# A two-block network on one core: how the conv half of a mixer layer gets its sum of squares

## The reference

```python
def rmsnorm(x, g):
    xf = x.astype(jnp.float32)
    y = xf * lax.rsqrt(jnp.mean(xf * xf, axis=-1, keepdims=True) + EPS)
    return (y * g.astype(jnp.float32)).astype(x.dtype)
...
        a = rmsnorm(h, mix_norm_g[i])
        proj = a @ w_in[i]
        q, k, v = (proj[..., 0:SB_WIDTH],
                   proj[..., SB_WIDTH:2 * SB_WIDTH],
                   proj[..., 2 * SB_WIDTH:3 * SB_WIDTH])
        off = 3 * SB_WIDTH
        u, c_gate, b_gate = (proj[..., off:off + CONV_WIDTH],
                             proj[..., off + CONV_WIDTH:off + 2 * CONV_WIDTH],
                             proj[..., off + 2 * CONV_WIDTH:off + 3 * CONV_WIDTH])
...
        qh = rmsnorm(heads(q), q_norm_g[i])
        kh = rmsnorm(heads(k), k_norm_g[i])
        vh = heads(v)
        attn = stick_breaking_attention(qh, kh, vh)
        attn = attn.transpose(0, 2, 1, 3).reshape(bsz, s_len, SB_WIDTH)

        conv = b_gate * causal_depthwise_conv(c_gate * u, conv_w[i], conv_b[i])

        mixed = jnp.concatenate([rmsnorm(attn, attn_out_g[i]),
                                 rmsnorm(conv, conv_out_g[i])], axis=-1)
        h = h + mixed @ w_o[i]
```

## Time and profile before

| | us |
|---|---|
| median of three runs | 1921.33 |
| lowest, highest | 1921.16, 1925.42 |
| the profiled execution, time | 1927.16 |
| the profiled execution, span | 1925.3 |
| PE busy in it | 1838.6 (95%) |
| DVE busy | 1395.7 (72%) |
| ACT busy | 1220.0 (63%) |

### The profile page before, as it was taken

One profiled execution on the slowest core, in us unless ns is written; L12 is line 12 of the kernel. 1 busy time (PEld: TensorE's weight loads), 2 busy tenths in 40 slices (PEclk: granted clock), 3 DMA queues, 4 the chain that ended last, 5 costly groups with the idle time before them and its releaser, 6 DMA issues.

```text
span 1925.3 us, 26803 instructions
## 1 busy us (share of the span) xinstructions
PE 1838.6 (95%) x9562; PEld 1546.2 (80%) x9562; DVE 1395.7 (72%) x1653; ACT 1220.0 (63%) x1536; POOL 5.9 (0%) x13
## 2 busy tenths in 40 slices
PE   8999979989999989879999999999999999999997
PEld 7877758979998779768878878788788787887885
DVE  4456755746664466458899898898998898989884
ACT  5545544644444455548687777786877777768773
POOL 0000000000000000000000000000000000000000
PEclk9889989999999999879999999999999999999999
DMA  9743223425445344219989899899898998998980
GB/s 321 248 165 109 74 102 131 154 100 190 177 190 202 111 175 176 93 67 339 369 319 362 317 364 364 310 367 355 325 361 319 352 360 325 358 345 343 357 323 23
DMA packets 68336, 483.32 MB, mean 251 GB/s; under 512 B 7610, under 2 KB 7738, under 8 KB 10928
## 3 DMA queue, kind: packets, MB, share of 16 engines
q1 hardware_dynamic: 66480, 475.26, 64.9%
q0 software_dynamic: 1792, 7.18, 1.8%
HBM read 478.22 MB, written 4.19 MB: 251 GB/s over the span
## 4 chain that ended last, share of the span: by engine, by line
PE 80%; DVE 8%; ACT 6%; issue 5%; DMA 0%; ACTq 0%; DVEq 0%; POOLq 0%
PE ps L1471 20%; PE ps L1472 19%; PE ps L1476 19%; DVE wlo L892 4%; PE ps L1716 4%; PE ps L1723 4%; PE ps L1717 4%; PE ps L1454 3%; ACT whi L549 2%; PE ps L1928 1%; PE ps L1929 1%; ACT xgh L846 1%; DVE sg L1015 1%; ACT sg L672 1%; PE ps L1819 1%
## 5 line engine op out<-in xcount | busy, mean ns | idle before, releaser
L892 DVE TENSOR_TENSOR wlo<-raw,whi 128x1024 fp32r<-128x1024 f32 x906 | 1044.1, 1212 | 171.8 <-ACT whi L549 171.3
L549 ACT ACTIVATE whi<-raw 128x1024 fp32r<-128x1024 f32 x906 | 904.2, 1055 | 154.6 <-PE ps L1476 127.4
L1471 PE MATMUL ps<-whi,xgh 128*128 128x512 f32 x896 | 360.2, 402 | 4.6 <-ACT whi L549 4.6
L1472 PE MATMUL ps<-whi,xgl 128*128 128x512 f32 x896 | 355.0, 396 | 0.0
L1476 PE MATMUL ps<-wlo,xgh 128*128 128x512 f32 x896 | 282.2, 396 | 0.0
L1471 PE MATMUL ps<-whi,xh 128*128 128x512 f32 (+1 forms) x448 | 186.9, 418 | 21.9 <-issue 9.9
L1471 PEld LDWEIGHTS ps<-whi,xgh 128*128 128x128 f32 x896 | 168.9, 188 | 43.1 <-ACT whi L549 4.8
L1476 PEld LDWEIGHTS ps<-wlo,xgh 128*128 128x128 f32 x896 | 168.9, 188 | 40.8
L1472 PEld LDWEIGHTS ps<-whi,xgl 128*128 128x128 f32 x896 | 169.2, 189 | 37.8
L1472 PE MATMUL ps<-whi,xl 128*128 128x512 f32 (+1 forms) x448 | 181.3, 406 | 0.0
L1471 PE MATMUL ps<-whi,mTh 128*128 128x512 f32 x448 | 178.3, 398 | 0.0
(11 more groups left out here) (288 smaller groups left out, 1902.5 us busy)
## 6 DMA issues: line engine op xcount, KB each, us to landing
raw<-in_w_moe_dram SPq DMA_DIRECT2D x336, 1024.0 KB, 6.7
raw<-in_w_fixed_dram SPq DMA_DIRECT2D x112, 1024.0 KB, 4.9
bias_scratch<-revb POOLq DMA_DIRECT2D x1, 3072.0 KB, 39.2
bias<-bias_scratch POOLq DMA_DIRECT2D x1, 2048.0 KB, 18.2
raw<-in_w_fixed_dram SPq DMA_DIRECT2D x4, 512.0 KB, 4.2
tok<-in_xt_dram SPq DMA_DIRECT2D x2, 512.0 KB, 4.5
h<-in_x_dram SPq DMA_DIRECT2D x1, 1024.0 KB, 13.6
out_dram<-h SPq DMA_DIRECT2D x2, 512.0 KB, 2.8
```

Source lines behind the costliest of these rows:

```text
L549: AC(whi[:, v % SPL, c], raw[:, v % RAW, c], ACT.Copy).then_inc(high_done, 1)
L892: V.tensor_tensor(wlo[:, v % SPL, c], raw[:, v % RAW, c], whi[:, v % SPL, c].bitcast(F32), ALU.subtract).then_inc(low_done, 1)
L1471: mm(o, hi(k0 + k, T), wh[:, k, :], start=first and k == 0, stop=False)
L1472: mm(o, lo(k0 + k, T), wh[:, k, :], start=False, stop=False)
```

## The change

DVE gets one more instruction per mixer layer. It adds up the four 128 x 256 tiles of conv squares to one tile `conv_squares` of 128 x 256, reading them with tokens outside and tiles inside (a step of 256 words, 1 KB, between the four values of one sum). It stands ahead of `low_part` on DVE, behind a wait for the squares. PE then sums this one tile over the features. The sums of the attention half stay as they are. `conv_squares` is a new buffer of 1 KB per partition, `conv_reduced` a new semaphore.

```diff
@@ -215,6 +215,7 @@
             sq = sb("sq", [P, NT, NB], scope=mx)
+            conv_squares = sb("conv_squares", [P, S], scope=mx)
...
@@ -312,6 +313,7 @@
         mix_sums = sem("mix_sums")
+        conv_reduced = sem("conv_reduced")
...
@@ -1274,6 +1276,9 @@
                 dve.wait_ge(conv_high, i + 1)
+                dve.wait_ge(mix_squares, 2 * i + 1)
+                V.tensor_reduce(conv_squares[:], mixs[:, KU:2 * KU].rearrange("p j n -> p n j"), AX, ALU.add)\
+                    .then_inc(conv_reduced, 1)
                 low_part(KU, 2 * KU, mixed, conv_low)
                 dve.wait_ge(mix_sums, 2 * i + 1)
                 V.tensor_copy(st[:, 24:26], ps[:, pair(B[f"o{i}"] + 1), 0:NT]).then_inc(conv_sums_copied, 1)
@@ -1835,12 +1840,12 @@
-                def sums(bank, j0):
+                def sums(bank, squares):
 
                     for T in range(NT):
-                        for j in range(j0, j0 + KU):
-                            ins = mm(ps[:, bank, T:T + 1], mixs[:, j, T * P:(T + 1) * P], ones[:, 0:1],
-                                     start=j == j0, stop=j == j0 + KU - 1)
+                        for j, s in enumerate(squares):
+                            ins = mm(ps[:, bank, T:T + 1], s[:, T * P:(T + 1) * P], ones[:, 0:1],
+                                     start=j == 0, stop=j == len(squares) - 1)
                     ins.then_inc(mix_sums, 1)
...
@@ -1861,9 +1866,9 @@
                 pv(0)
                 scores(1)
-                pe.wait_ge(mix_squares, 2 * i + 1)
-
-                sums(pair(B[f"o{i}"] + 1), KU)
+                pe.wait_ge(conv_reduced, i + 1)
+
+                sums(pair(B[f"o{i}"] + 1), [conv_squares[:]])
                 pe.wait_ge(conv_low, i + 1)
                 project(0)
                 pe.wait_ge(conv_sums_copied, i + 1)
@@ -1873,7 +1878,7 @@
-                sums(7, 0)
+                sums(7, [mixs[:, j] for j in range(KU)])
                 project(2)
```

## The result

| | before | after |
|---|---|---|
| median of 16 runs each, us | 1923.78 | 1929.45 |
| lowest, highest | 1920.85, 1927.2 | 1925.06, 1934.73 |
| the profiled execution, time | 1927.16 | 1930.32 |
| its span | 1925.3 | 1928.2 |

The ratio is 1.0027, with a 95% interval of 1.0017 to 1.0036: the change costs 3.3 to 6.9 us, some 5.2. The forecast was +4.0 us (ratio 1.0021) and no change by the bound of 0.3%. The forecast stood on a median before of 1921.33 us; the ratio carries that to 1926.5 us, inside the range of 1921.2 to 1929.3. (The median after as it stands, 1929.45, goes with a median before of 1923.78.)

What follows compares the result with a forecast made beforehand. The prediction took PE to bound the kernel. Later starts of 2.36 us plus one more clock fall of 1.63 us gave +3.99 us on 1921.33 us: 1925.3 us, range 1921.2 to 1929.3 for 8 in 10.

Steps and rivals of the forecast that it cites:

- The bound: Whole kernel: the chain of waits follows PE; at the sums it goes ACT, ACT, PE, with DVE not in it.
- The 12 passes saved bring nothing: PE's sums ahead of project(0): 12 of 16 passes fewer, 1.33 us per mixer, but inside a wait, so no gain.
- The reduction's length: New DVE reduction: 1.22 us, taken from the reduction of q and k squares; bounds 748 ns and 2.15 us.
- nearer 2 us: Sign against the forecast: the DVE reduction takes nearer 2 us than the 1.22 us assumed.
- The later start: project(0) waits for DVE's reduction and xl behind the square: +1.18 us per mixer, 2.36 us for two.
- What is free: Work queued behind DVE's new wait (copy of sums, weight split, softplus(1), reload) costs nothing; 2.3 us remain before softplus(1).
- The clock: TensorE's clock behind project(0)'s start: falls in both mixers, one fall more than the profile before, +1.63 us.
- rival 2: Stepped reduction at 2.15 us, clock low twice as long in both mixers: 9.1 us more, 1930.4 us; chance 0.08 in full.
- stepped read with one more fall: Reduction slowed by its stepped read, only one more clock fall: +5.8 us, 1927.2 us, on the 0.3% bound; chance 0.09.
- Rival 1: The wait ahead of project(0) alone costs, clock falls as often as before: +2.36 us, 1923.7 us; chance 0.25.
- rival 4: Clock behind project(0)'s later start falls in neither mixer: +0.7 us, 1922.1 us; chance 0.07.
- rival 3: PE's 12 passes of the sums come off the path: 2.7 us less, 1918.7 us; chance 0.01.

Runs made afterwards that it cites:

- r7_late8: Kernel before, its 8 products of the sums moved to the middle of project(0), no reduction on DVE; ratio 1.000 to before.
- r4_late: Changed kernel with the reduction behind the xl instructions on DVE and the sums in the middle of project(0); ratio 0.9977 to before.
- r5_forms: Kernel before plus four unused stepped or side-by-side reductions and a copy in DVE's idle time; reductions 1.21 us side by side, 1.91 us with 1 KB step.
- r1_wait: Kernel before with only one wait more: DVE's xl of the conv half also waits for ACT's square, no reduction; ratio 1.000.
- r2_adds: Changed kernel with two side-by-side additions in place of the one stepped reduction, same place on DVE; ratio 1.0018 to before.
- r3_fill: Changed kernel with 12 unused 512-column products on PE ahead of the wait for the reduced squares and 4 behind the sums; ratio 1.0022 to before.
- r6_late_fill: r4_late with unused 512-column products on PE, 6 ahead of pv(1) and 11 behind it; ratio 0.9947 to before, 1913.41 us.
- x4_fill: r3_fill as it is, profiled once more, one run only; 1924.61 us.

## Why the prediction was right, and where it was off

*The bound.* PE's chain, with DVE out of it before and in it after: right. The predicted chain (`xh`, square, reduction, `xl`, PE) is the measured one, piece by piece. In the prediction's list of what would show it, "2.95 us or so" does not agree with its own 376.67 - 373.65 = 3.02 us; measured are 3.67 us (369.38 to 373.05).

*The 12 passes saved bring nothing.* Right: the 4 passes lie between two waits of PE. r7_late8 against r4_late shows what they are worth when they do lie on the path, 1.3 us per mixer against the 1.33 us worked out.

*The reduction's length.* This is the first term that was mis-sized: 1.22 us taken, 1.93 us measured. The prediction had named a reduction "nearer 2 us" as a sign of being wrong, and that sign came. The length stood between its bounds (0.75 and 2.15 us), but the row nearest by name and number of words was the wrong one. The upper bound scaled the whole row of `cbias`, its fixed part too. (Nor is that row the slowest per word: `xgl`, L1401, takes 342 ns for 128 words, 2.7 ns a word, for the same reason.) An estimate without the fixed part: reductions that read side by side take 1220 ns for 1024 words and 653 ns for 480 (L975 of the kernel before), so 1.04 ns a word and some 0.15 us fixed; `cbias` is then (1.008 - 0.15) / 480 = 1.79 ns a word, and 1024 words 1.98 us. That this comes so near is in part luck: `cbias` is a copy that writes with a step, and r5_forms's copy that reads with one takes 1.18 us for 1024 words.

The Trainium skill's sentence on 16-byte lines ("SBUF — State Buffer", section "Door 1: The DMA port swizzle") pointed the right way: 1.91 us with a step against 1.21 us without for the same words. The steps tried were 64 bytes and 1 KB, so where the penalty begins, at 16 bytes or elsewhere, no run here shows. What that skill's page "VectorE: DVE Perf Modes" says of Mode 1× (section "Mode 1× (REGULAR) — the baseline"), that it works for any stride and gives one result a cycle, is not borne out by this read if it is taken to mean the same time for any stride, as the prediction took it.

*The later start.* +1.18 us forecast, +1.81 us measured: the difference is the reduction's (0.71 us more), less 0.08 us, since `xl` starts while the reduction's last 0.08 us run. The way from the square over DVE to PE was right, and r1_wait and r2_adds confirm it at two other lengths: with 0, 1.06 and 1.85 us on DVE between the square and `xl`, `project(0)` starts 4.50, 5.53 and 6.31 us after `xh`. A microsecond on DVE is one on the path, from the point on where the sums' products stop covering it (in r1_wait, 0.09 us to spare).

*What is free.* Right, each of it: the copy of the sums, the split and `softplus(1)` all came in time. `softplus(1)` still waits for ACT:

```profile
377.15 1.76 DVE L1220 SCALAR_TENSOR_TENSOR spb<-ps,spa 128x1536 f32<-128x1536 f32 x1 [1.83 <-ACT spa L777]
```

The 3.33 us of idle time in the earlier trace rows became 1.83 us (forecast 2.3).

*The clock.* Right in kind: a fall in both mixers where before had one, 1.63 us for the new one. This is the second term that was mis-sized, by 1.30 us, since in the second mixer the low stretch doubled. That was only in rival 2. r3_fill shows the cause of the falls: with PE at work in the same waits both are gone. Why the second mixer's is the longer one stays open.

*The sum.* 2.36 + 1.63 = 3.99 us was forecast; the profiles have 3.62 + 2.93 = 6.55 us, the runs 5.2 us (3.3 to 6.9). Both terms came out larger than forecast, by 1.26 and 1.30 us, so that 3.99 us lies inside the runs' interval is owed to that interval's width and in part to luck, and not to a sum that came out. The outcome lies between the forecast and rival 2; by the number it is nearest to the case "stepped read with one more fall" (+5.8 us), to which I gave 0.09, but what happened is the stepped read with one long fall. That case stood only in a half sentence of rival 2, without a chance, and its limit there was worked out wrongly: by the prediction's own terms one more fall and one twice as long (3.26 us) pass 0.3% from a reduction of 1.3 us on, not 1.9. The profiles' 6.55 us are indeed above that limit of 5.8 us, the runs' 5.2 us below it. So "no change by 0.3%" held by 0.6 us, and the interval reaches beyond it (1.0036). The bound was also wider than it had to be: with 16 runs each the interval is 0.1% to either side, and tells this change from none. *Rival 1* (no more falls) and *rival 4* (fewer) are out by three profiles of the changed kernel, *rival 3* by the chain.

## What to carry to other kernels

Work taken off the critical engine can be worth less than nothing if what replaces it stands in a queue ahead of something that the same engine waits for next; look at the second wait, not only the first. Put the cheap substitute behind the urgent instruction, and ask for its result as late as the program allows. A wait of TensorE costs its length and, where little work surrounds it, can cost a second time in the clock of the products behind it (here 1.6 to 2.9 us a fall). Products whose results nobody uses, 16 per mixer in r3_fill and 17 in r6_late_fill, held the clock there. Count the whole program afterwards: in r3_fill a fall came up in another place and took 1.5 us back.

## What the hardware showed that I had not expected

- A float32 reduction on DVE over 1024 words takes 1.21 us with the words side by side and 1.88 to 1.93 us with a step of 64 bytes or 1 KB. A copy of 1024 words read with a 1 KB step takes 1.18 us, where the nearest single-source row without a step has 748 ns.
- The same stepped reduction takes 1.93 us while PE stands still (all three profiles of the changed kernel), and 2.01 to 2.05 us beside PE's products (r4_late, r6_late_fill, r3_fill, x4_fill). ACT is busy throughout in both cases. `xl`, which reads side by side, keeps its 1.65 to 1.67 us beside PE's products in r3_fill. Whether it is PE's reading or its writing was not tried.
- 16 one-column passes fill 1.8 us on PE in the records. Behind 0.84 us of idle time and these passes the clock fell in the second mixer of before and stayed up in the first; behind the same passes in the middle of products it stayed at 1.00 in both (r7_late8). With 16 products of 512 columns in r3_fill's waits it stayed up too.
- These falls sit at the same places in each profile of a kernel, within half a microsecond measured from the start of `project(0)`, though the time of an execution varies by 6 us and more. In the changed kernel they begin up to 0.6 us ahead of that start, in the kernel before 1.2 us behind it.
